# Retention in another order, its head norms inside the delta rule, and an output projection that begins with these heads

## What is computed

```python
def retention_chunkwise(q, k, v, log_gamma):
    ...
    inner = jnp.einsum('nbhij,nbhjv->nbhiv', jnp.einsum('nbhid,nbhjd->nbhij', qc, kc) * decay, vc)
    def step(R, xs):
        q_c, k_c, v_c = xs
        o = jnp.einsum('bhik,bhkv->bhiv', q_c * xi[..., None], R)
        R = g_chunk * R + jnp.einsum('bhjk,bhjv->bhkv', k_c * zeta[..., None], v_c)
        return R, o
...
def head_group_norm(t, g):
    mu = jnp.mean(t, axis=-1, keepdims=True)
    var = jnp.mean(jnp.square(t - mu), axis=-1, keepdims=True)
    return (t - mu) * lax.rsqrt(var + NORM_EPS) * g.astype(jnp.float32)
...
    o_gdn = rms_norm(o_f + o_b, gdn_norm_g) * jax.nn.silu(z.reshape(b, tl, N_HEADS_GDN, HEAD_DIM))
...
    o_ret = head_group_norm(r_f + r_b, ret_norm_g) * jax.nn.silu(rg.reshape(b, tl, N_HEADS_RET, HEAD_DIM))
```

## Time and profile before

| | us |
|---|---|
| median of 3 runs | 3481.64 |
| lowest, highest | 3481.49, 3484.16 |
| the profiled execution | 3481.5 |
| its span (first to last instruction) | 3479.7 |

### The profile page before, as it was taken

One profiled execution on the slowest core, in us unless ns is written; L12 is line 12 of the kernel. 1 busy time (PEld: TensorE's weight loads), 2 busy tenths in 40 slices (PEclk: granted clock), 3 DMA queues, 4 the chain that ended last, 5 costly groups with the idle time before them and its releaser, 6 DMA issues.

```text
span 3479.7 us, 46745 instructions
## 1 busy us (share of the span) xinstructions
PE 3375.9 (97%) x17274; PEld 2844.0 (82%) x17274; DVE 1236.5 (36%) x1890; ACT 1367.0 (39%) x1910; POOL 1484.2 (43%) x1090
## 2 busy tenths in 40 slices
PE   6999899899999999999999999999999999999998
PEld 4777799788888888888888888888888888888887
DVE  6763577521123111645216111331126353151104
ACT  4444333544325432326524443254323264244423
POOL 2232000255544554454543554455544545545544
PEclk9999999999999999999999999999999999999999
DMA  6342000122222222222222322222222323223222
GB/s 259 127 146 67 1 1 1 67 97 96 97 97 91 96 96 97 86 98 94 100 96 73 109 96 97 85 97 96 96 97 91 98 85 108 94 72 108 96 97 97
DMA packets 90036, 322.21 MB, mean 93 GB/s; under 512 B 9776, under 2 KB 12208, under 8 KB 89776
## 3 DMA queue, kind: packets, MB, share of 16 engines
q1 hardware_dynamic: 88576, 316.64, 26.9%
q10 hardware_dynamic: 1328, 3.67, 0.3%
HBM read 318.18 MB, written 2.10 MB: 92 GB/s over the span
## 4 chain that ended last, share of the span: by engine, by line
issue 55%; POOL 33%; PE 10%; DVE 1%; POOLq 1%; ACT 0%; DMA 0%; DVEq 0%; SPq 0%; ACTq 0%
POOL w_lo L456 33%; PE ps L485 2%; PE ps L481 2%; PE ps L480 2%; PE ps L994 1%; PE ps L999 1%; PE ps L992 1%; PE ps L1018 0%; PE ps L1022 0%; PE ps L1016 0%; POOLq L454 0%; DVE X L2002 0%; POOLq L123 0%; PE ps L937 0%; DVE ps L2024 0%
## 5 line engine op out<-in xcount | busy, mean ns | idle before, releaser
L456 POOL TENSOR_TENSOR w_lo<-raw,w_hi 128x512 fp32r<-128x512 f32 x1086 | 1484.0, 1388 | 1987.2 <-ACT w_hi L1164 1987.1
L1164 ACT ACTIVATE w_hi<-raw 128x1024 fp32r<-128x1024 f32 x543 | 575.5, 1060 | 1459.6 <-PE ps L485 897.8
L480 PE MATMUL ps<-acts,w_hi 128*128 128x512 f32 x2776 | 1080.1, 389 | 0.1
L481 PE MATMUL ps<-acts,w_hi 128*128 128x512 f32 x2776 | 1080.0, 389 | 0.0
L485 PE MATMUL ps<-acts,w_lo 128*128 128x512 f32 x2776 | 685.6, 389 | 0.0
L480 PEld LDWEIGHTS ps<-acts,w_hi 128*128 128x128 f32 x2776 | 521.1, 188 | 108.4 <-ACT tmp L1518 0.5
L485 PEld LDWEIGHTS ps<-acts,w_lo 128*128 128x128 f32 x2776 | 521.1, 188 | 108.1
L481 PEld LDWEIGHTS ps<-acts,w_hi 128*128 128x128 f32 x2776 | 521.2, 188 | 108.0
L2072 DVE TENSOR_TENSOR tmp<-tmp,ps 128x512 f32<-128x512 f32 x110 | 75.7, 688 | 787.6 <-PE ps L485 727.4
L992 PE MATMUL ps<-acts,w_hi 128*128 (+1 forms) x440 | 171.2, 389 | 0.0
L994 PE MATMUL ps<-acts,w_hi 128*128 (+1 forms) x440 | 171.2, 389 | 0.0
(11 more groups left out here) (382 smaller groups left out, 4123.6 us busy)
## 6 DMA issues: line engine op xcount, KB each, us to landing
raw<-stream SPq DMA_DIRECT2D x543, 512.0 KB, 3.3
ada_behind<-ada SPq DMA_DIRECT2D x32, 512.0 KB, 3.6
ada_first<-ada SPq DMA_DIRECT2D x8, 1024.0 KB, 13.3
X<-x_in ACTq DMA_DIRECT2D x1, 2048.0 KB, 8.4
out<-X SPq DMA_DIRECT2D x16, 128.0 KB, 1.8
xin<-x_in ACTq DMA_DIRECT2D x2, 768.0 KB, 6.9
xin<-x_in SPq DMA_DIRECT2D x2, 768.0 KB, 9.0
rope_sb<-rope SPq DMA_DIRECT2D x1, 1280.0 KB, 9.0
```

The source lines that it names most:

```text
L456: last = nc.gpsimd.tensor_tensor(w_lo[:, slot, part, :], raw[:, slot % RAW, part, :], f32(w_hi[:, slot, part, :]), ALU.subtract)
L480: mm(o, w_hi[:, s, k, :], xh, start=start, stop=False, skip_group_check=True)
L481: mm(o, w_hi[:, s, k, :], xl, start=False, stop=False, skip_group_check=True)
L1164: A(w_hi[:, s, :, :], raw[:, s % RAW, :, :], ACT.Copy).then_inc(s_hi, 1)
```

## The change

- SP loads the two small constants before `ada_first`, and the three larger ones only after the third chunk of weights (`s_fixed`). PE makes the sums of squares after 6 pieces of the modulation instead of 8. ACT copies two of the four rows of the second part (`s_arow2`).
- In the item loop the rows of a part are copied one item earlier, ahead of that item's convolution.
- The transposes of ab (`turn_ab`) stand behind the first two token tiles of the values, whose order is now 2, 3, 0, 1, 4, 5.
- Retention: ACT copies each value tile when it is done and scales keys in between. POOL makes the decayed queries, between two low parts. PE's order is new: the next query-key products stand ahead of the other direction's outputs, in two banks in turn, and the delta rule's decay rows and key products stand inside the retention's last steps. ACT copies the first outputs out of PSUM in place of DVE.
- Delta rule: the retention heads' sums are in step 0, their centring and squares in step 1, their Ln, Exp and results in step 5. The masked products of both directions stand ahead of the right sides. The two sets of buffers `gts` change places, and `hn` lies elsewhere.
- The output projection starts when the last outputs are added to `ogdn`; the squares of the delta heads are summed (`delta_squares`) after its second head.

The number of products doesn't change. The diff, cut to its core:

```diff
             for k in (0, 2):
                 sp.dma_start(xin[:, k:k + 2, :], x_in[:, k:k + 2, :]).then_inc(s_xin, 16)
-            load_first(0)
-            load_first(1)
             sp.dma_start(ident[:, :], consts[:, 0:P]).then_inc(s_cst, 16)
             sp.dma_start(ones[:, :], consts[:, P:2 * P]).then_inc(s_cst, 16)
-            for n in range(2, FIRST):
+            for n in range(FIRST):
                 load_first(n)
-            sp.dma_start(cst1[:, :, :].rearrange("p a n -> p (a n)"), consts[:, 2 * P:5 * P]).then_inc(s_cst, 16)
...
                 load_chunk(n, n % RAW)
+                if n == 2:
+                    sp.dma_start(cst1[:, :, :].rearrange("p a n -> p (a n)"), consts[:, 2 * P:5 * P]).then_inc(s_fixed, 16)
...
+            with rounds(pool, N_PROJ // SLOTS, (hi, SLOTS)):
+                for slot in range(SLOTS):
+                    low_part(slot)
+            for slot in range(SLOTS - 1 + N_PROJ % SLOTS):
+                low_part(slot % SLOTS)
+            pool.wait_ge(s_fin, n_aux[-1])
+            pool.wait_ge(s_sil, 3 * H)
+            pool.wait_ge(s_dexp, 1)
+            decayed_queries(NCC)
+            low_part((N_PROJ + SLOTS - 1) % SLOTS)
+            for s in range(NCC + 1, NC):
+                decayed_queries(s)
...
+            for n in range(KT - 2):
+                part_chunk(n, 0)
+            pe.wait_ge(s_cst, 32)
             pe.wait_ge(s_sqadd, KT)
             mm(ps[4][:, 0:CTX], ones[:, :], big[2][:, 0:CTX], start=True, stop=True)
             mm(ps[5][:, :], ones[:, :], big[2][:, CTX:TOK], start=True, stop=True).then_inc(s_ss, 1)
-            for n in range(KT, KT + 4):
+            for n in range(KT - 2, KT + 4):
                 part_chunk(n, n // KT)
             turn_part(0, 6)
...
-            pe.wait_ge(s_pread, len(items))
+            def turn_ab():
...
+            pe.wait_ge(s_pread, len(items) - 1)
             pe.wait_ge(s_aux_read, n_aux[len(items) - 1])
...
+                for n, t in enumerate((2, 3, 0, 1, 4, 5) if q == 0 else range(NC)):
+                    if (q, n) == (0, 2):
+                        turn_ab()
...
+                    elif q == H - 1:
+                        last.then_inc(s_rvt, 1)
...
+            pe.wait_ge(s_rv, 4)
+            pe.wait_ge(s_turned, 2 * NC - 1)
+            for s in range(2):
+                key_values(s, 0)
+                key_values(s, 1)
+                turn(2 * NC + 2 * s)
+                turn(2 * NC + 2 * s + 1)
+            pe.wait_ge(s_rv, NC)
+            query_keys(NCC)
+            for s in range(NCC, NC):
+                outputs(s, 0)
+                if s < NC - 1:
+                    key_values(s, 0)
+                    query_keys(s + 1)
+                outputs(s, 1)
+                if s < NC - 1:
+                    key_values(s, 1)
+                if s == NCC:
+                    turn(2 * NC + 4)
+                    turn(2 * NC + 5)
+                if s == NCC + 1:
+                    pe.wait_ge(s_turned, len(turned))
+                    decay_rows(0)
+                if s == NCC + 2:
+                    key_products(0)
+            def ret_sums(first):
+                if first:
+                    pe.wait_ge(s_hm, first)
+                for h in (first, first + 1):
+                    mm(ps[4 * (h % 2) + 2][:, :], ones[:, :], oret[:, h, :], start=True, stop=True).then_inc(s_hsum, 1)
+            def ret_squares(first):
+                pe.wait_ge(s_hrsq, first + 2)
+                if first:
+                    pe.wait_ge(s_hvar, first)
+                else:
+                    pe.wait_ge(s_rhs, 2)
+                for h in (first, first + 1):
+                    mm(ps[4 * (h % 2) + 2][:, :], ones[:, :], tmp[h][:, :], start=True, stop=True).then_inc(s_hss, 1)
...
                         if lev == 6:
+                            if s == 1:
+                                pe.wait_ge(s_hvar, H)
...
+                    if s == 0 and lev in (2, 4):
+                        ret_sums(lev - 2)
+                    if s == 1 and lev in (4, 5):
+                        ret_squares(2 * (lev - 4))
...
+                        if s == 0 and lev == 1:
+                            pe.wait_ge(s_ro[d], NC - NCC)
...
-            pe.wait_ge(s_go[0], 4)
-            pe.wait_ge(s_go[1], 4)
-            for h in range(H):
-                mm(ps[4 + h][:, :], ones[:, :], oret[:, h, :], start=True, stop=True).then_inc(s_hsum, 1)
...
+            def delta_squares():
+                for h in range(H):
+                    pe.wait_ge(s_hsq, h + 1)
+                    mm(ps[h][:, :], ones[:, :], hq[:, h, :], start=True, stop=True).then_inc(s_hss, 1)
...
                     pe.wait_ge(low, n.now)
                     for j in range(SLOTS):
                         high_low(j, k)
+                    if k == 1 and second:
+                        second()
...
-            opening(FIRST_OUT[:4], s_yh, s_y, n_y)
+            pe.wait_ge(s_go[0], 4)
+            pe.wait_ge(s_go[1], 4)
+            opening(FIRST_OUT[:4], s_yh, s_y, n_y, second=delta_squares)
...
+            act.wait_ge(s_acol, 1)
+            act.wait_ge(s_ada, 2 * KT)
+            for q in (2, 3):
+                last = A(arow[0:2, 2 * P * q:2 * P * (q + 1)], ps[1][32 * q:32 * q + 2, 0:2 * P], ACT.Copy)
+            last.then_inc(s_arow2, 1)
...
+            for _ in range(H - 1):
+                done()
+            for t in range(NC):
+                if t < NC - 1:
+                    act.wait_ge(s_rvt, t + 1)
+                else:
+                    act.wait_ge(s_done, used.up())
+                A(rvtok[:, t, :], ps[t][:, :], ACT.Copy).then_inc(s_rv, 1)
+                if t in (2, 4):
+                    scaled_keys(t // 2 - 1)
+            hi_part()
+            scaled_keys(2)
+            scaled_keys(3)
+            first_outputs(NCC, 0)
+            first_outputs(NCC, 1)
+            scaled_keys(4)
+            first_outputs(NCC + 1, 0)
+            first_outputs(NCC + 1, 1)
...
+            act.wait_ge(s_turned, len(turned))
+            def ret_head_squares():
+                for d in range(2):
+                    act.wait_ge(s_ro[d], 4)
+                for h in range(H):
+                    A(tmp[h][:, :], oret[:, h, :], ACT.Square).then_inc(s_hrsq, 1)
+            def ret_mean_squares():
+                act.wait_ge(s_hm, 2 * H)
+                for h in range(H):
+                    A(hn[h], hn[h], ACT.Square).then_inc(s_hm2, 1)
...
+                    if s == 0 and lev == 2:
+                        ret_head_squares()
+                    if s == 1 and lev == 2:
+                        ret_mean_squares()
+                    if s == NC - 1 and lev < 5:
+                        for h in (0, 1) if lev % 2 else (2, 3):
+                            (head_log if lev < 3 else head_factor)(h)
+                    if s == NC - 1 and lev == 5:
+                        head_operand(0)
...
+            for j in range(1, H):
+                head_operand(j)
...
-                if i in TURNS:
-                    part_rows(TURNS[i], 6)
+                if i < n and items[i][0] in CONV + ROPED:
+                    dve.wait_ge(s_pread, i + 1)
+                if i + 1 in TURNS:
+                    part_rows(TURNS[i + 1], 6)
...
-            unit(0)
+            def ret_means(first):
+                for h in (first, first + 1):
+                    dve.wait_ge(s_hsum, h + 1)
+                    TS(hn[h], ps[4 * (h % 2) + 2][:, :], -1.0 / P, None, ALU.mult).then_inc(s_hm, 1)
+            def ret_centred():
+                dve.wait_ge(s_hm, H)
+                dve.wait_ge(s_hrsq, H)
+                for h in range(H):
+                    TT(oret[:, h, :], oret[:, h, :], hn[h], ALU.add).then_inc(s_hm, 1)
+            def ret_variances(first):
+                for h in (first, first + 1):
+                    dve.wait_ge(s_hss, h + 1)
+                    dve.wait_ge(s_hm2, h + 1)
+                    STT(tmp[h][:, :], ps[4 * (h % 2) + 2][:, :], 1.0 / P, hn[h], ALU.mult,
+                        ALU.subtract).then_inc(s_hvar, 1)
...
+            for s in range(NCC, NC - 1):
+                for d in range(2):
+                    if s > NCC + 1:
+                        added_outputs(s, d)
+                    new_state(s, d)
+                    if d == 0:
+                        masked_products(s + 1)
+                if s == NCC:
+                    copy_turn(2 * NC + 4)
+                    copy_turn(2 * NC + 5)
+                if s == NCC + 1:
+                    for d in range(2):
+                        dve.wait_ge(s_rkz[d], NC - 1)
+                    unit(0)
...
+            dve.wait_ge(s_rod[0], NC - NCC)
+            turned_pairs(0, 0)
+            dve.wait_ge(s_rqx[1], NC - NCC)
+            turned_pairs(0, 1)
             for d in range(2):
-                turned_pairs(0, d)
+                added_outputs(NC - 1, d)
...
-                        if s and lev == 2 + d:
```

(23 more changed lines are left out.)

306 lines of the change are left out of this document (146 added, 160 removed).

## The result

| | us |
|---|---|
| kernel before, median of 4 runs | 3481.8 (3481.5 to 3484.2) |
| changed kernel, median of 4 runs | 3424.7 (3423.3 to 3426.4) |
| ratio, with its 95% interval | 0.9835 (0.9818 to 0.9852) |
| changed kernel, the profiled execution and its span | 3426.35, 3424.5 |

The changed kernel is 57 us faster. The forecast was 49.4 us faster, 3432, in a range of 3424 to 3444, so the direction and the range held, the range by 0.7 us, and the gain was 7.7 us larger than forecast. The 3427 to 3437 that the main case was good for did not hold.

What follows compares the result with a forecast made beforehand. PE, busy 97% of the span, was taken as the bound; savings were waits and half-clock time. Terms −0.3 − 5.5 − 1.8 − 30.6 + 7.0 − 18.2 = −49.4 took 3481.6 to 3432.2 us, range 3424 to 3444.

Steps and rivals of the forecast that it cites:

- main case: Whole kernel: forecast 3432 us, itself good for 3427 to 3437, chance 0.60.
- Start: Up to the first product: 2.5 us gained, less DVE meeting POOL's low parts; net gain 0.3 us.
- Rows and narrow transposes: Items and value projection: earlier row copies gain 5.5 us, last item's transposes behind two value tiles gain 1.8.
- Retention: Value projection's end to delta rule level 2: 66.8 us becomes 36.2, gain 30.6, with the clock at full.
- the 1.0 for small waits: Retention: 1 us allowed for small waits within the 36.2 us.
- Delta rule: Eight added products, DVE delays and relief from DVE's order: sum +7.0 us, bounds +3 and +10.
- relief by DVE's order: Delta rule: every second 0.5 us wait for L1877 and most of three 1.0 us waits for L1814 go, −4.4 us.
- Norms and output projection: Last delta product to next chunk's first product: 45.2 us becomes 27.0, gain 18.2, bounds 14 and 19.5.
- the 1.0 for the clock: Output projection: 1.0 us added for a clock that may fall after the 2.7 us wait in front.
- The clock did not fall in the retention steps: Rival: clock falls in the retention steps again, costing up to 9 us, 3438 to 3441; chance 0.15.
- paid in full: Rival: DVE becomes the delta rule's bound and the 4.4 us relief does not come, 3439; chance 0.13.
- the better case: Rival: the start gains its 2.5 us and the small waits don't appear, 3428; chance 0.09.

Runs made afterwards that it cites:

- old order: Changed kernel with DVE's order inside the delta rule put back (masked query-key products at level 2, second right side at level 3): 3435.2 us.
- rows back: Changed kernel with the modulation's row copies again behind the previous item's convolution: 3429.2 us.
- double sums: Changed kernel with each of the eight sums over the retention heads inside the delta rule issued twice: 3430.8 us.
- queries on DVE: Changed kernel with the retention heads' decayed queries made on DVE, not POOL: 3425.7 us.
- low parts later: Changed kernel where POOL begins its low parts only when the first normed operand is whole: 3426.4 us.
- squares early: Changed kernel with the retention heads' sums of squares and variances one level earlier in the delta rule's second step: 3424.6 us.
- additions first: Changed kernel with the last two additions to `ogdn` ahead of DVE's results of retention heads 2 and 3 and head 1's low part: 3422.1 us.
- the order alone: Kernel before with DVE's new order inside the delta rule and nothing else: 3473.9 us.
- masked products early: Kernel before with only both directions' masked query-key products moved from level 2 to level 1: 3478.8 us.
- queries on POOL: Kernel before with only the retention heads' decayed queries moved from DVE to POOL: 3473.1 us.

## Why the prediction was right, and where it was off

**Start.** Right: 0.24 us for a forecast of 0.3. DVE is free for the operand's coefficients (L1751) 2.44 us earlier, at 38.23 and not 40.67, for a forecast of 2.5. Then these and three instructions of the operand meet POOL's, at 0.75 to 0.95 us each; before, one did in full and the coefficients by 0.2. That takes 2.5 us more than before, within the 1.8 to 2.7 of the forecast. The run with later low parts confirms price and cause. The Trainium skill ("SBUF — State Buffer", "Who interferes with whom") says that the second of the two fully blocks; my sum by it took a whole POOL instruction for each meeting and a loss of 1.7 us. A POOL instruction takes 1.3 us there (5.17 for four, from 37.86), and here the measurement decides for the smaller price. The rule itself may hold, where DVE's instruction comes when POOL's is already under way; the rows don't show when it was issued.

**Rows and narrow transposes.** Right: both waits are gone, 6.9 us in the trace against 7.3. A new wait of 0.6 us for ACT (at L506) is in that. Putting the rows back cost 5.8 us in the trace, 6.3 from the wait on.

**Retention.** The size was right, 35.2 us for a forecast of 36.2, and so was the assumption that the clock stays at 1.00. The two waits forecast as 0.9 and 1.0 us were 0.78 and 0.66, and of the 1.0 for small waits nothing came. The reason given for the waits on L1786, that they go because POOL makes these products, was only half of it. With DVE making them in the new order they are gone as well, at 1.4 us. There DVE makes each query a half step earlier, and PE has other products in between; which of the two removes the waits is not shown, though the 2.5 us to spare speak for the first. POOL alone removes them as well, in the old order. Either would have done it; the forecast priced them together and so didn't notice.

**Delta rule.** The direction of each part was right but one, and the sizes were off by 6 us together:

| Part | forecast | measured |
|---|---|---|
| eight products and the waits in steps 0 and 1 | +9.0 | +7.8 |
| relief by DVE's order, steps 2 to 4 | −4.4 | −7.9 |
| last step | +0.6 | −0.7 |

The first row is 3.25 us in step 0 and 4.52 in step 1. The merge that was to be 0.4 us late there was not, and the wait for the variances was 0.91 us, not 1.3. The step that failed is the relief. It said that the new order takes away every second wait for L1877 (three of 0.5 us) and most of the three for L1814. The runs showed that all nine in steps 2 to 4 go. The six short ones, with what else the masked products held up, are worth 4.8 us and not 1.5; the three merge waits are 3.1, near their listed size and near the 2.9 that the sum leaves for them. The order helps the last step too: with it alone this one is 1.0 us shorter. The head results in it cost about 0.3 us, not 0.6. The row to read would have been the step as a whole: 40.71 us in the kernel before for products that need 38.1.

**Norms and output projection.** Right: 16.0 us for 16.4. The wait was 2.27 us, against 2.7 with the pipe's 0.87, and the opening took 26.9 us from its first product to the next chunk, for a forecast of 26.1 (its 21.4 for 96 multiplies is 20.9 by its own row). The operands of the delta heads were in time: PE doesn't wait for one. What was too small is the 1.0 for the clock. It fell, and cost 1.6. Where the clock stays up the opening takes 25.3 us, for 25.1 in the forecast without that term.

**Rivals.** The clock did not fall in the retention steps, nor was the spreading "paid in full" in the rival's sense. Its eight products are paid, but the relief came too, and nearly twice. The nearest case was the better one, 3428, and even that lacked the relief. That the range held is in part luck: its lower end was drawn for the better case, and the miss in the relief left 0.7 us of it.

## What to carry to other kernels

A wait in a list of waits can be a lower bound: two of 0.5 us, one ahead of each half of a group, cost 1.5 us here, while one of 1.0 us between whole groups cost 1.0. So a repeated step should be priced by its whole length against the sum of its groups at full pitch. Two edits that remove the same wait (another engine for the late result, and an earlier place for it) don't add up, and to give each its credit takes a run with one and without the other. A wait moved away from a queue that is itself full comes back elsewhere, as the squares, the low parts and the additions did; what holds is an order in which the late result is simply made before the one that nobody waits for yet.

## What the runs showed of the hardware

The same wait costs a different amount from trace to trace. Seven traces have the wait of 2.27 us ahead of the output projection with identical work behind it. In four of them (the changed kernel, old order, rows back, double sums) the granted clock then falls to its lower level for some microseconds (0.68 as the mean from 582.0 to 587.4 us in the changed kernel), and the opening takes 26.8 to 26.9 us; in three (queries on DVE, low parts later, squares early) it stays at 1.00, and the opening takes 25.3. PE does the same products in the last step before the wait in all of them. In the three traces with the additions first, which have a wait of 0.83 us there and one of 0.82 to 0.87 at the squares behind it, the clock is 1.00 all through. What decides between the two in the seven is open. These 1.6 us are as much as the medians of the small experiments differ by.

The kernel before has such a chance at its start. In its own trace the scaling of x began at 30.36 us and took 7.04, and the first product came at 44.80. In the trace with the order alone it began later and met POOL's first low parts:

```profile
31.77 9.19 DVE L1633 TENSOR_TENSOR xin<-xin,big 128x768 f32<-128x768 f32 x8 [5.65 <-ACT big L1187]
...
36.86 6.44 POOL L456 TENSOR_TENSOR w_lo<-raw,w_hi 128x512 fp32r<-128x512 f32 x4 [36.41 <-ACT w_hi L1164]
...
47.37 0.80 PE L536 MATMUL ps<-h,w_hi 128*128 128x512 f32 x1 [3.39 <-DVE h L1652]
```

The first product is at 47.4 us there, and at 47.6 and 47.4 in the two other traces of this start (masked products early, queries on POOL). In these two the items take 3 us longer as well, with a granted clock of 0.98 from 190 to 320 us, and PE reaches the retention at 343.9 us, against 338.1 in the kernel before's own trace and 341.0 with the order alone. In the changed kernel the scaling is over at 34.4 us, before POOL begins. So the changed start is worth 0.2 us against the profiled execution and 2.8 to 3.0 against these, and which of them is the usual case for the kernel before is not shown.
